# Turning the pages of keys on VectorE instead of TensorE in a hybrid decoder step

## The reference

```python
def stick_breaking_block(q_blk, q_pos, k, v, k_pos, bias):
    z = (jnp.einsum('bqhd,bkhd->bhqk', q_blk.astype(jnp.float32), k.astype(jnp.float32)) * (SB_HEAD_DIM ** -0.5)
         + bias.astype(jnp.float32)[None, :, None, None])
    mask = k_pos[None, :] < q_pos[:, None]
    log_not = jnp.where(mask, jax.nn.log_sigmoid(-z), 0.0)
    between = lax.cumsum(log_not, axis=3, reverse=True) - log_not
    a = jnp.where(mask, jnp.exp(jax.nn.log_sigmoid(z) + between), 0.0)
    return jnp.einsum('bhqk,bkhd->bqhd', a, v.astype(jnp.float32))
```

## Time and profile before

| | |
|---|---|
| runs | 2360.7, 2364.34, 2367.49 us |
| median | 2364.34 us |
| profiled execution | 2363.2 us, span 2361.5 us, mean granted clock 0.988 |
| stage of the key rounds | 1228 to 1379.1 us |
| stage of the value rounds | 1379.1 to 1504 us |

### The profile page before, as it was taken

One profiled execution on the slowest core, in us unless ns is written; L12 is line 12 of the kernel. 1 busy time (PEld: TensorE's weight loads), 2 busy tenths in 40 slices (PEclk: granted clock), 3 DMA queues, 4 the chain that ended last, 5 costly groups with the idle time before them and its releaser, 6 DMA issues. The chain is left out here.

```text
span 2361.5 us, 47384 instructions
## 1 busy us (share of the span) xinstructions
PE 2272.0 (96%) x18644; PEld 2019.1 (86%) x18644; DVE 1644.3 (70%) x2774; ACT 1057.1 (45%) x1919; POOL 48.9 (2%) x108
## 2 busy tenths in 40 slices
PE   7999999999999999999969999899999999999998
PEld 7999999987879888888858866578999999997786
DVE  7766766656885487677657898657676766655886
ACT  7322222234554667566645555435522323233453
POOL 0000000000000100000010001010000000000000
PEclk9999999999999999999979999899999999999999
DMA  5343333365463233233258878723243432437454
GB/s 161 103 137 117 108 128 102 116 214 187 134 187 108 63 75 69 54 59 74 37 153 294 277 254 310 235 79 118 59 159 102 130 121 87 151 116 237 128 166 153
DMA packets 356274, 328.40 MB, mean 139 GB/s; under 512 B 103929, under 2 KB 264057, under 8 KB 356112
## 3 DMA queue, kind: packets, MB, share of 16 engines
q1 hardware_dynamic: 356112, 326.16, 44.5%
HBM read 254.63 MB, written 71.47 MB: 138 GB/s over the span
## 5 line engine op out<-in xcount | busy, mean ns | idle before, releaser
L1242 PE MATMUL a_q<-a_uh,a_p_hi 128*128 128x352 f32 x672 | 233.6, 348 | 0.6 <-ACT a_xp L1333 0.6
L1244 PE MATMUL a_q<-a_uh,a_p_lo 128*128 128x352 f32 x672 | 216.6, 322 | 0.0
L1243 PE MATMUL a_q<-a_ul,a_p_hi 128*128 128x352 f32 x672 | 216.1, 322 | 0.0
L1242 PEld LDWEIGHTS a_q<-a_uh,a_p_hi 128*128 128x128 f32 x672 | 126.6, 188 | 23.5 <-issue 21.6
L1243 PEld LDWEIGHTS a_q<-a_ul,a_p_hi 128*128 128x128 f32 x672 | 127.1, 189 | 0.1
L1244 PEld LDWEIGHTS a_q<-a_uh,a_p_lo 128*128 128x128 f32 x672 | 126.2, 188 | 0.0
L884 PE MATMUL c_q<-c_b_hi,c_a_hi 128*128 128x512 f32 x264 | 105.4, 399 | 3.9 <-DVE c_a_lo L783 3.0
L884 PE MATMUL a_q<-a_b_hi,a_a_hi 128*128 128x512 f32 x264 | 103.7, 393 | 3.2 <-DVE a_a_lo L783 3.0
L885 PE MATMUL c_q<-c_b_hi,c_a_lo 128*128 128x512 f32 x264 | 104.7, 396 | 0.0
L886 PE MATMUL c_q<-c_b_lo,c_a_hi 128*128 128x512 f32 x264 | 104.6, 396 | 0.0
L886 PE MATMUL a_q<-a_b_lo,a_a_hi 128*128 128x512 f32 x264 | 102.9, 390 | 0.0
(11 more groups left out here) (735 smaller groups left out, 7635.9 us busy)
## 6 DMA issues: line engine op xcount, KB each, us to landing
b_page<-in_cache_k SPq DMA_DIRECT2D x128, 256.0 KB, 4.2
b_page<-in_cache_v SPq DMA_DIRECT2D x128, 256.0 KB, 4.3
a_w_raw<-in_ffn_gu SPq DMA_DIRECT2D x44, 512.0 KB, 5.1
c_w_raw<-in_ffn_gu SPq DMA_DIRECT2D x44, 512.0 KB, 5.0
a_a_raw<-hid_rows SPq DMA_DIRECT2D x66, 256.0 KB, 2.7
c_a_raw<-hid_rows SPq DMA_DIRECT2D x66, 256.0 KB, 2.7
a_p_raw<-in_w_in SPq DMA_DIRECT2D x28, 512.0 KB, 4.2
a_raw_d<-in_ffn_d SPq DMA_DIRECT2D x11, 1024.0 KB, 5.0
```

The lines of the kernel that those rows point to most:

```text
L1242: nc.tensor.matmul(self.pm[at % 2][:, 0:TB], wh, self.uh[t][:, c], start=(c == 0), stop=False)
L1243: nc.tensor.matmul(self.pm[at % 2][:, 0:TB], wh, self.ul[t][:, c], start=False, stop=False)
L1244: mm = nc.tensor.matmul(self.pm[at % 2][:, 0:TB], wl, self.uh[t][:, c], start=False, stop=(c == KC - 1))
```

## The change

SP now loads a key page onto 32 partitions: sequence b of the group goes to partitions 32b to 32b + 31, and each partition holds four successive tokens, 8 KB in one piece (value pages are loaded as before). VectorE transposes this in blocks of 32x32, by four instructions of 128x512 each round. TensorE's transposes and both engines' copies of keys are gone, and with them three uses of PSUM banks. After the block transposes a partition holds the columns of one sequence: of each 64-column head 32 at a time. So the score product is reordered: 16 products again, each with queries of all four sequences in a block form (`q_in`, 16 blocks of 32 columns, built in the unused rows of `mixed`) and with keys whose innermost step is 512 numbers. One column block of the result now holds two heads of four sequences, where it held eight heads of one sequence. The masks, the bias and the copy of the weights follow this new order. ScalarE now brings the scores to `ex`, with the bias in the same instruction. The queries are stored in a second form, `q_blocks`, by four DMAs in the first half, and loaded by four more at the beginning of this function. TensorE waits for queries and masks at its first score product and not at the beginning. The due times are the same, under new names.

The diff, cut to its core:

```diff
+                if kind == "query":
+                    sp.dma_start(self.q_blocks[:, 4 * hp:4 * hp + 4, :].rearrange("r j n -> j r n"), ring[hp % 2][:, T_P:T]).then_inc(self.E(f"cols_out{hp % 2}"), 16)
...
-        qs, ks = s.sb("qs", [P, 4, T_S]), s.sb("ks", [P, 4, T_S])
+        ks = s.sb("ks", [P, 4, T_S])
         k_turned = [s.sb("k_turned", [P, 4, 4, P])[:], w_early[:].rearrange("p r (b c n) -> p (r b) c n", b=2, n=P)]
         ex = s.sb("ex", [P, G, KEYS])
         run = s.sb("run", [P, KEYS])
-        qb = s.sb("qb", [P, G, 4, 4, R])
+        q_block, qs = run[:, 0:512].rearrange("p (j n) -> p j n", n=T_S), run[:, 512:640].rearrange("p (c n) -> p c n", n=T_S)
+        q_own = s.sb("q_own", [P, G, 4, R])
+        q_in = mixed[:, NT, :].rearrange("p (g j n) -> p g j n", g=G, n=R)
...
-        pk, pz, pw = [S0, S1, S4], [S2, S3], [S2, S3]
+        pz, pw = [S2, S3], [S2, S3]
...
-            sp.dma_start(qs[:], q_cols.rearrange("c p n -> p c n")).then_inc(E("q_cols_in"), 16)
+            sp.dma_start(qs, q_cols.rearrange("c p n -> p c n")).then_inc(E("q_cols_in"), 16)
+            for b in range(4):
+                sp.dma_start(q_block[rows_in(b)], q_blocks).then_inc(E("q_cols_in"), 16)
...
-                        sp.wait_ge(E("k_turned1"), 2 * old + 2)
+                        sp.wait_ge(E("k_turned"), 4 * old + 4)
...
-                        sp.dma_start(page[:, n % SLOTS, b:b + 1, :], src.rearrange("g p n -> p g n")).then_inc(E(f"page_in{n % SLOTS}"), 16)
+                        if keys:
+                            sp.dma_start(page[rows_in(b), n % SLOTS].rearrange("p s n -> p (s n)"),
+                                         src.rearrange("g (t s) n -> t (g s n)", s=4)).then_inc(E(f"page_in{n % SLOTS}"), 16)
+                        else:
+                            sp.dma_start(page[:, n % SLOTS, b:b + 1, :], src.rearrange("g p n -> p g n")).then_inc(E(f"page_in{n % SLOTS}"), 16)
...
-            made(nc.gpsimd.memset(qb[:], 0.0))
+            made(nc.gpsimd.memset(q_own[:], 0.0))
+            made(nc.gpsimd.memset(q_in, 0.0))
             pool.sem_inc(E("qb_zero"), 1)
-            for m in (pick_t, own_t, sample_t):
-                made(nc.gpsimd.memset(m[:], 1.0))
+            for m in (pick_t[:], bias_t, own_t[:], sample_t[:]):
+                made(nc.gpsimd.memset(m, 1.0))
...
+            for c in range(4):
+                select(bias_t[:, rows_in(c)], 2 * c, -1, [[0, 4], [1, 2], [0, L_S]], ALU.is_equal)
...
-            def turn_keys():
-                for n, (gi, p) in enumerate(KEY_ROUNDS):
-                    for half in range(2):
-                        yield key_time(gi, p) + PE_AT["turn_keys"][half]
-                        if half == 0:
-                            pe.wait_ge(E(f"page_in{n % SLOTS}"), 64 * (n // SLOTS) + 64)
-                        for e in range(2):
-                            b = 2 * half + e
-                            q = 4 * n + b - 3
-                            at_least(pe, E(f"k_copied{q % 2}"), q // 2 + 1)
-                            for c in range(4):
-                                mm = nc.tensor.transpose(pk[(4 * n + b) % 3][:, c], page[:, n % SLOTS, b, c * P:(c + 1) * P], ident[:])
-                            mm.then_inc(E(f"k_turned{e}"), 1)
-
-            def products(out, gi, moving):
+            def block_scores(out, gi, n):
+
+                keys = k_turned[n % 2].rearrange("p b c n -> p (b c n)").rearrange("p (s j t) -> p j t s", s=4, t=R)
+                for j in range(4):
+                    for c in range(4):
+                        mm = nc.tensor.matmul(out[rows_in(c), 0:P], q_in[:, gi, 4 * c + j], keys[:, 4 * c + j], start=(j == 0), stop=(j == 3))
+                mm.then_inc(E("z_mm"), 1)
+
+            def own_scores(out, gi):
 
                 for c in range(4):
-                    for b in range(4):
-                        mm = nc.tensor.matmul(out[R * b:R * b + R, :], qb[:, gi, c, b], moving(b, c), start=(c == 0), stop=(c == 3))
+                    mm = nc.tensor.matmul(out[rows_in(c), 0:T_S], q_own[:, gi, c], ks[:, c], start=True, stop=True)
                 mm.then_inc(E("z_mm"), 1)
 
             def scores():
                 for r, (gi, p) in enumerate(ALL_ROUNDS):
                     yield key_time(gi, p) + PE_AT["scores"][0]
                     at_least(pe, E("z_out"), r - 1)
-                    if p < PAGES:
-                        for e in range(2):
-                            pe.wait_ge(E(f"k_copied{e}"), 2 * (PAGES * gi + p) + 2)
-                        products(flat(pz[r % 2])[:, 0:P], gi, lambda b, c: k_turned[(PAGES * gi + p) % 2][:, b, c])
+                    if r == 0:
+                        pe.wait_ge(E("masks_out"), 1)
+                        pe.wait_ge(E("q_ready"), 1)
+                    n = PAGES * gi + p
+                    if p == PAGES:
+                        own_scores(flat(pz[r % 2]), gi)
                     else:
-                        products(flat(pz[r % 2])[:, 0:T_S], gi, lambda b, c: ks[:, c])
+                        pe.wait_ge(E("k_turned"), 4 * n + 4)
+                        block_scores(flat(pz[r % 2]), gi, n)
...
-            def key_copies():
-                for n, (gi, p) in enumerate(KEY_ROUNDS):
-                    for half in range(2):
-                        yield key_time(gi, p) + ACT_AT["key_copies"][half]
-                        if half == 0 and n >= 2:
-                            act.wait_ge(E("z_mm"), turned_free(n))
-                        act.wait_ge(E("k_turned0"), 2 * n + half + 1)
-                        nc.scalar.activation(k_turned[n % 2][:, 2 * half], pk[(4 * n + 2 * half) % 3][:], ACT.Copy).then_inc(E("k_copied0"), 1)
+            def logits():
+                for r, (gi, p) in enumerate(ALL_ROUNDS):
+                    keys = P if p < PAGES else T_S
+                    yield key_time(gi, p) + ACT_AT["logits"][0]
+                    if r == 0:
+                        act.wait_ge(E("masks_out"), 1)
+                    act.wait_ge(E("z_mm"), r + 1)
+                    nc.scalar.activation(ex[:, gi, p * P:p * P + keys], flat(pz[r % 2])[:, 0:keys], ACT.Identity, bias=row_bias[:]).then_inc(E("z_out"), 1)
...
-                    nc.scalar.activation(wt[0:keys, r % 2, :], flat(pw[r % 2])[0:keys, 0:P], ACT.Copy).then_inc(E("wt_copied"), 1)
+                    nc.scalar.activation(wt[0:keys, r % 2, :].rearrange("p (b c x) -> p c b x", b=4, c=4),
+                                         flat(pw[r % 2])[0:keys, 0:P].rearrange("p (c b x) -> p c b x", c=4, b=4), ACT.Copy).then_inc(E("wt_copied"), 1)
...
-            def key_copies():
+            def turn_keys():
                 for n, (gi, p) in enumerate(KEY_ROUNDS):
-                    for half in range(2):
-                        yield key_time(gi, p) + DVE_AT["key_copies"][half]
-                        if half == 0 and n >= 2:
+                    for z in range(4):
+                        yield key_time(gi, p) + DVE_AT["turn_keys"][z // 2]
+                        if z == 0 and n >= 2:
                             dve.wait_ge(E("z_mm"), turned_free(n))
-                        dve.wait_ge(E("k_turned1"), 2 * n + half + 1)
-                        nc.vector.tensor_copy(k_turned[n % 2][:, 2 * half + 1], pk[(4 * n + 2 * half + 1) % 3][:]).then_inc(E("k_copied1"), 1)
-
-            def logits():
-                for r, (gi, p) in enumerate(ALL_ROUNDS):
-                    keys = P if p < PAGES else T_S
-                    yield key_time(gi, p) + DVE_AT["logits"][0]
-                    dve.wait_ge(E("z_mm"), r + 1)
-                    nc.vector.tensor_scalar(ex[:, gi, p * P:p * P + keys], flat(pz[r % 2])[:, 0:keys], row_bias[:], None, ALU.add).then_inc(E("z_out"), 1)
+                        if z == 0:
+                            dve.wait_ge(E(f"page_in{n % SLOTS}"), 64 * (n // SLOTS) + 64)
+                        nc.vector.transpose(k_turned[n % 2][:, z].rearrange("p c n -> p (c n)"), page[:, n % SLOTS, z]).then_inc(E("k_turned"), 1)
...
-            dve.wait_ge(E("q_cols_in"), 16)
+            dve.wait_ge(E("q_cols_in"), 80)
             for gi in range(G):
-                for h in range(H_SB):
-                    c, e = h // 2, h % 2
-                    src = qs[e * DH:(e + 1) * DH, c, 16 * gi:16 * gi + 16].rearrange("p (b q) -> p b q", q=L_S)
-                    step = nc.vector.tensor_copy(qb[e * DH:(e + 1) * DH, gi, c, :, L_S * h:L_S * h + L_S], src)
-                step.then_inc(E("q_ready"), 1)
+                for e in range(2):
+                    half = slice(e * DH, (e + 1) * DH)
+                    src = qs[half, :, 16 * gi:16 * gi + 16].rearrange("p c (b q) -> p c b q", q=L_S)
+                    nc.vector.tensor_copy(q_own[half, gi].rearrange("p c (b x) -> p c b x", b=4)[:, :, :, L_S * e:L_S * e + L_S], src)
+                    for b in range(4):
+                        k, at_ = rows_in(b), 2 * L_S * b + L_S * e
```

(3 more changed lines are left out.)

42 lines of the change are left out of this document (20 added, 22 removed).

## The result

The changed kernel takes 2396.07 us, the median of 4 runs (2393.38 to 2397.05), against 2364.04 for the kernel before beside it: ratio 1.0134, 95% interval 1.0116 to 1.0151. It is 32 us slower. The profiled execution has a span of 2395.3 us.

What follows compares the result with a forecast made beforehand. TensorE was taken to bound the keys' stage before, VectorE after; 6.7 (VectorE) + 2.8 (beginning) + 3.0 (clock) = 12.5 us on 2363.2 gave 2375.7, stated as 2376 us, range 2366 to 2400.

Steps and rivals of the forecast that it cites:

- The bound before: Keys' stage of the kernel before: TensorE bounds it, busy 144.8 of 151.1 us.
- VectorE, +6.7 us: Keys' stage: VectorE's 146.0 us of work plus 11.8 of waits make 157.8 against 151.1 us.
- The new wait: Keys' stage: VectorE's queue now waits for key pages to land; four page buffers cover it, cost nothing.
- The rival: Keys' stage: page transfers become the bound because each load fills only 32 partitions; 2388 us, chance 0.31.
- The rival's price: Transfers as bound of the keys' stage: 2400 us in full at 198 GB/s, taken as 2388; decides below 243 GB/s.
- The stride: Score products reading keys 2 KB apart: decides only from 3.3 times their price; 2395 us at four times, chance 0.05.
- The beginning, +2.8 us: Start of the keys' stage: four more query loads, 1.6 us, and more query copies, 1.2 us; between 0 and 3.5.
- The clock, +3.0 us: Keys' stage: TensorE, busy 48%, gets a clock of 0.7, so VectorE's waits for it grow; bounds 0 and 7.4.
- the waits I had kept: Keys' stage: 11.8 us of VectorE's waits, nearly all in the chunk chain, assumed to remain after the change.
- the forecast's case: Whole run: VectorE takes TensorE's place as the bound at a slightly slower pace, 2376 us, chance 0.50.

Runs made afterwards that it cites:

- before_logits: Kernel before, with only the 34 additions of the bias (logits) moved from VectorE to ScalarE: 2364.7 us, against 2364.0 for the kernel before.
- wide_loads: Changed kernel with the old loads of key pages, over all 128 partitions with 2 KB each: 2367.2 us.
- the comb: Changed kernel with each key page loaded onto 64 alternate partitions, even or odd, with 4 KB each: 2368.8 us.
- wide_close: Changed kernel with key pages loaded over all 128 partitions and score products reading adjacent key columns instead of 2 KB apart: 2363.2 us.
- Five_turns: Changed kernel with key pages loaded over 128 partitions, plus a fifth, unused 128x512 transpose on VectorE each key round: 2383.1 us.
- after: The changed kernel itself, with the whole change, against the kernel before: 2396.1 us, ratio 1.0116 to 1.0151.

## Why the prediction was right or wrong

**The bound before: right, as far as the runs show.** TensorE is busy for 96% of the keys' stage; before_logits took 9 us from VectorE there, and nothing came of it.

**VectorE, +6.7 us: right once the loads are wide, its sum in part by luck.** The transposes take 79.7 us in union, with wide loads 82.0 (forecast 81.5; 0.61 apart, forecast 0.64). With wide loads the stage takes 158.1 us, with the comb 157.5, forecast 157.8. The parts were 149.8 busy and 8.4 waits, not 146.0 and 11.8: 3.8 too little and 3.4 too much, which offset one another. Without the stride (wide_close) VectorE is busy for 144.8. Five_turns shows that VectorE bounds the stage there.

**The new wait, "Cost nothing at the present rate": this step failed.** It rested on the median landing of one load, 4.2 us, and on four buffers that cover it, three rounds of 4.9 us. Two things are wrong with that. The landing was that of the old loads; under the new ones it is 11.7 us. And a landing is the wrong measure: 11.7 us would still fit into the 14.7 of three rounds. Buffers cover a delay, they don't raise a rate. The pages alone, 33.6 MB, take 146 us at the 230 GB/s measured, and with the stage's other 8 MB at the same rate it is 181 us, 5.7 a round, where VectorE needs 4.9. The term is 29 us (after against wide_loads), with 27 us of it in the stage. Of these, waits that end with a landing are 17.5 us; the rest is waits elsewhere, which shrink as well once the loads are wide (8.4 us of idle time in all). The rival was there with the right mechanism, the right place and the right sign (idle ahead of the first transpose of a round, share near 1, low GB/s), and got 0.31.

**The rival's price: better at its full size than as I put it.** Its test was a rate below 243 GB/s; the rate is 228. The full price, 2400, came from 5.3 us a round for pages and 20 us for the other 8 MB at the best rate. Both were off and in part offset one another. All of the stage's 276 x 151.1 = 41.7 MB move at 228 GB/s, 183 us: the pages faster than at my 198 GB/s (219 to 230), the other rows much slower than at 396, as they share the transfers' time with the narrow loads. With 2388 I had cut the price in half for want of a row, not from one. The row which I set for it (192 KB on 32 partitions in 2.8 us) is the landing of one transfer and says nothing of a rate with many behind one another. The Trainium skill's figure, which I had in a sentence beside the sum, gave 4.8 us a round, and with the other 8 MB at the same rate it would have come to an estimated 41.7 MB / 218 = 191 us, against the 185 of the stage. The prediction put those 8 MB at full speed.

**The stride: no bound, but not free.** The products cost 2.1 times their price, below my 3.3, and TensorE is not the bound. Its busy time was far off, though: 76.6 us forecast, 128.7 measured in the changed kernel, 70% of the stage and not about half. The products take 75.5 us in place of 35.5, and the rest goes with a granted clock of 0.88 in place of 0.97. Still wide_close is 4.0 us faster than wide_loads. The cost arrives through VectorE (last section).

**The beginning, +2.8 us:** the gates' sums are taken up at 1230.6 us against 1228.0, +2.6; but the traces scatter by as much as that. The four traces with the old beginning lie between 1226.8 and 1229.3 (mean 1228.2), the ten with the new one between 1228.5 and 1230.9 (mean 1229.9). The term is about 1.7 us, within its bounds and below the 2.8.

**The clock, +3.0 us: not seen.** In the changed kernel the granted clock is 0.88, in wide_loads 0.93, in wide_close even 0.77, which is the fastest of the three. The term would have to be in the time in which VectorE isn't busy: that is 8.4 us in wide_loads and 8.4 in wide_close, the same at either clock, and 3.4 less than the waits I had kept.

**Where it all went.** Stage +34, beginning +2.6, behind the function 3 less, which is what the two traces of the kernel before differ by: together the 33.8 us between the spans, 2361.5 and 2395.3. Of the 32 us in the medians 29 are the narrow loads and 3 the rest. The forecast 2376 has the wrong size because its likeliest case left out the largest term; the range held the time. Without that term the forecast's case was too high: wide_loads takes 2367.2 us and not 2376. Its keys' stage is 7 us longer, as forecast, but its beginning costs 1.8, the clock nothing, and behind the function its trace is 6 us shorter than the first of before, 3 than the second.

## What to carry to other kernels

When a change gives a transfer another shape, the rates and landings in the trace of before no longer hold for it; look for a row with the new shape and many transfers in a row, and where there is none, weigh the full price seriously if the stage already has a DMA share as high as the 0.82 here. Compare rates and not landings: buffers hide a delay, but not a queue that needs 5.7 us for what is used up in 4.9. Look at which partitions a load reaches, not at how many bytes its rows have: on this chip 64 alternate partitions did as well as 128, and 64 neighbouring ones no better than 32. In this kernel, block transposes on VectorE put each sequence on 32 partitions of its own, and the price was narrow loads; that cost more than TensorE's 512 transposes, whose removal freed an engine that VectorE did not let finish earlier.

## What the runs showed of the hardware

**Strided reads by TensorE slow VectorE.** wide_loads and wide_close differ only in the order in which TensorE reads the turned keys. In the first VectorE is busy for 149.8 us of the keys' stage, in the second for 144.8, with the same instructions. Two of VectorE's groups, up to 1384 us, wide_loads first:

```profile
L3129 DVE STREAM_TRANSPOSE b_k_turned<-b_page 128x512 f32<-128x512 f32 x64 | 41.8, 711 | 1.2 <-PE b_S L2736 0.7 <-DVE m_rkd L3017 0.4
...
L3052 DVE TENSOR_TENSOR b_dec<-b_dec,m_masks 128x512 f32<-128x512 f32 x4 | 3.6, 893 | 0.1
```

```profile
L3129 DVE STREAM_TRANSPOSE b_k_turned<-b_page 128x512 f32<-128x512 f32 x64 | 39.6, 675 | 1.6 <-PE b_S L2736 1.2 <-DVE m_rkd L3017 0.4
...
L3052 DVE TENSOR_TENSOR b_dec<-b_dec,m_masks 128x512 f32<-128x512 f32 x5 | 3.4, 675 | 0.1
```

Their means are 675 ns with ordered reads, 711 and 893 with strided ones. The single instructions of one trace show it too: in wide_loads the 58 transposes of 128x512 that overlap a strided product in time take 734 ns on average, the other 70 take 674; in wide_close it is 677 and 674. The 5.0 us of busy time match the 4.9 us by which the stage is shorter. Why the reads of one engine slow the other, no run shows.

**The step costs each engine something else.** At the full clock float32 products with a step of 2 KB in their moving operand take 2.1 to 2.2 times as long (16 products of 128 columns: 2.24 us in the median of the changed kernel's rounds, 2.40 of wide_loads', against 1.08). At 1.2 GHz the difference is smaller: 2.3 to 2.5 us in the few rounds that there are, against 1.9. A block transpose that writes 16 bytes apart takes 1.6 times as long (1070 against 680 ns).

**A DMA share near 1 is no sign of a high rate.** 0.98 at 228 GB/s in the changed kernel, 0.78 at 261 in wide_loads: the share says that the engines have work, the GB/s what comes of it.
